# Attention scores as one fp32 product per head, and no splitting of q and k on GpSimd

## The reference

```python
def dilated_window_attention(q, k, v, window, dilation):   # q, k after rotary; 16 heads of 64
    r = window // (2 * dilation)                            # 64 for all three patterns
    # tokens are taken with a stride of `dilation`, each query sees keys at a distance <= 64 of them
    scores = jnp.einsum('nbqhd,nbkhd->nbhqk', qb, kw) * (HEAD_DIM ** -0.5)
    ...
    lse = jax.nn.logsumexp(scores, axis=-1)
    p = jnp.exp(scores - lse[..., None])
    o = jnp.einsum('nbhqk,nbkhd->nbqhd', p, vw)
    return o, lse

def dilated_mixture(q, k, v):
    # (window, dilation) = (128, 1), (512, 4), (2048, 16); merged with a softmax over the three lse
    ...
```

## Time and profile before

| What | us |
|---|---|
| median of three runs | 4509.62 |
| the profiled execution, its own time | 4508.95 |
| its span (first to last instruction) | 4507.3 |
| PE busy in the span | 4045.8 |
| POOL busy in the span | 1849.8 |
| attention, first to last score of TensorE | 2761.5 to 3883.2 |

### The profile page before, as it was taken

One profiled execution on the slowest core, in us unless ns is written; L12 is line 12 of the kernel. 1 busy time (PEld: TensorE's weight loads), 2 busy tenths in 40 slices (PEclk: granted clock), 3 DMA queues, 4 the chain that ended last, 5 costly groups with the idle time before them and its releaser, 6 DMA issues. The chain is left out here.

```text
span 4507.3 us, 61424 instructions
## 1 busy us (share of the span) xinstructions
PE 4045.8 (90%) x22213; PEld 3098.9 (69%) x22213; DVE 2337.4 (52%) x4451; ACT 1289.4 (29%) x3501; POOL 1849.8 (41%) x1135
## 2 busy tenths in 40 slices
PE   7999999999999999856777775999999999699999
PEld 5887778887788877623333334777777777588887
DVE  4402624205344026066888884666666666465654
ACT  1011220012120112101222223566566666422222
POOL 5453355443454533348999994111321121100000
PEclk9999999999999999978888887999999999899999
DMA  4232243231342322262222224334333343444442
GB/s 157 96 106 77 76 132 103 91 101 58 107 129 94 108 76 78 73 244 97 88 89 88 88 86 106 89 102 109 96 98 82 91 111 94 137 151 165 150 161 104
DMA packets 332021, 483.51 MB, mean 107 GB/s; under 512 B 27771, under 2 KB 228547, under 8 KB 329731
## 3 DMA queue, kind: packets, MB, share of 16 engines
q1 hardware_dynamic: 300867, 365.58, 25.5%
q0 software_dynamic: 26304, 94.78, 7.2%
q10 hardware_dynamic: 4608, 19.92, 1.3%
HBM read 315.04 MB, written 165.15 MB: 107 GB/s over the span
## 5 line engine op out<-in xcount | busy, mean ns | idle before, releaser
L253 POOL TENSOR_TENSOR front_w_hi<-front_w_raw,one 128x1024 fp32r<-128x1024 f32 (+1 forms) x168 | 302.6, 1801 | 932.9 <-PE front_out L475 920.4
L1487 ACT ACTIVATE attn_p_sb<-attn_p_sb,attn_o_sb 128x256 f32<-128x256 f32 (+1 forms) x1152 | 535.4, 467 | 388.1 <-DVE attn_o_sb L1520 388.1
L1520 DVE CUSTOM_DVE_ANT_0 attn_p_sb<-attn_s_ps,attn_mask 128x256 f32<-128x256 f32 (+1 forms) x1152 | 388.0, 374 | 91.1 <-PE attn_s_ps L1421 46.1
L256 POOL TENSOR_TENSOR front_w_lo<-front_w_raw,front_w_hi 128x1024 fp32r<-128x1024 f32 (+1 forms) x168 | 410.3, 2442 | 13.2
L406 DVE TENSOR_SCALAR front_acc<-front_chan,front_consts 128x1024 f32<-128x1024 f32 (+2 forms) x36 | 38.9, 1080 | 714.2 <-ACT front_chan L296 714.2
L475 PE MATMUL front_out<-front_h_hi,front_w_hi 128*128 128x512 f32 x1392 | 359.0, 401 | 8.9 <-DVE front_turned L386 3.6
L1421 PE MATMUL attn_s_ps<-attn_k_hi,attn_q_hi 64*128 64x256 f32 (+1 forms) x1152 | 283.6, 489 | 74.6 <-POOL attn_k_lo L1324 46.7
L475 PE MATMUL front_out<-front_h_hi,front_w_lo 128*128 128x512 f32 x1392 | 346.6, 391 | 0.0
L475 PE MATMUL front_out<-front_h_lo,front_w_hi 128*128 128x512 f32 x1392 | 344.2, 389 | 0.0
L1434 PE MATMUL attn_pt_ps<-ident,attn_p_sb 128*128 128x128 f32 x1920 | 339.9, 292 | 4.3 <-ACT attn_p_sb L1487 1.2
L960 PE MATMUL ssd_seg<-ssd_spread,masks 128*128 128x512 f32 x384 | 252.4, 800 | 95.5 <-POOL ssd_spread L899 95.4
(11 more groups left out here) (183 smaller groups left out, 7525.6 us busy)
## 6 DMA issues: line engine op xcount, KB each, us to landing
front_w_raw<-w_in POOLq DMA_DIRECT2D x156, 512.0 KB, 4.2
s_o<-attn_o_sb SPq DMA_DIRECT2D x288, 132.0 KB, 2.0
output_parts<-s_o SPq DMA_DIRECT2D x24, 1584.0 KB, 6.6
back_xb<-s_xb ACTq DMA_DIRECT2D x24, 640.0 KB, 6.3
ssd_xb<-s_xb SPq DMA_DIRECT2D x24, 640.0 KB, 3.9
s_q<-front_stage SPq DMA_DIRECT2D x48, 256.0 KB, 2.2
s_k<-front_stage SPq DMA_DIRECT2D x48, 256.0 KB, 2.3
s_zs<-front_stage SPq DMA_DIRECT2D x48, 256.0 KB, 3.5
```

The costliest lines, as they stand in the source:

```text
L253: nc.gpsimd.tensor_tensor(hi, raw, one.to_broadcast([P, 2, cols]), ALU.mult).then_inc(sem["w_hi_ready"], 1)
L256: nc.gpsimd.tensor_tensor(lo, raw, hi.bitcast(F32), ALU.subtract).then_inc(sem["w_split"], 1)
L1487: last = nc.scalar.activation(cut, cut, ACT.Exp, scale=-1.0, bias=o_sb[g // 2 % ring][:, g % 2, h, VW:OW], accum_out=o_sb[g // 2 % ring][: ...
L1520: last = nc.vector.tensor_tensor_reduce(out=p_sb[g % 3][:, h, 0:width], in0=s_ps[g % 2][h][:, 0:width], in1=mask[:, step.pattern.strip(ste ...
```

## The change

The score of a head becomes one fp32 product of q and k. The tiles `q_hi`, `q_lo`, `k_hi`, `k_lo` become `q` and `k`, the 192 split instructions on POOL and their two semaphores go, and TensorE waits, at the first step of a visit, for the 8 loads of q and k in place of the last split.

```diff
-        q_hi = [mem.sbuf(f"q_hi{u}", [P, longest], F32R) for u in range(2)]
-        q_lo = [mem.sbuf(f"q_lo{u}", [P, longest], F32R) for u in range(2)]
-        k_hi = [mem.sbuf(f"k_hi{u}", [P, longest + 2 * REACH], F32R) for u in range(2)]
-        k_lo = [mem.sbuf(f"k_lo{u}", [P, longest + 2 * REACH], F32R) for u in range(2)]
+        q = [mem.sbuf(f"q{u}", [P, longest]) for u in range(2)]
+        k = [mem.sbuf(f"k{u}", [P, longest + 2 * REACH]) for u in range(2)]
...
         def _(pool):
             for u in range(2):
-                for t in (k_hi[u], k_lo[u]):
-                    for at in (0, REACH + SEQS[1]):
-                        nc.gpsimd.memset(t[:, at:at + REACH].bitcast(F32), 0.0).then_inc(sem["a_pads_set"], 1)
+                for at in (0, REACH + SEQS[1]):
+                    nc.gpsimd.memset(k[u][:, at:at + REACH], 0.0).then_inc(sem["a_pads_set"], 1)
...
-            for part in range(len(split_parts(1))):
-                split(0, part)
             for step in steps:
-                following = step.visit + 1
-                if following < len(visits) and 0 <= step.at - 12 < len(split_parts(visits[following][0])):
-                    split(following, step.at - 12)
...
                 else:
-                    sp.wait_ge(sem["a_pads_set"], 8)
-                for name, tile, at in (("q", q_lo[u], 0), ("k", k_lo[u], REACH)):
+                    sp.wait_ge(sem["a_pads_set"], 4)
+                for name, tile, at in (("q", q[u], 0), ("k", k[u], REACH)):
...
                 if step.first_of_visit:
                     if step.visit == 0:
-                        pe.wait_ge(sem["a_pads_set"], 8)
-                    pe.wait_ge(sem["a_low"], splits_before(step.visit + 1))
+                        pe.wait_ge(sem["a_pads_set"], 4)
+                    pe.wait_ge(sem["a_qk_in"][u], 16 * 8 * (step.visit // 2 + 1))
...
-                for x, (qs, ks) in enumerate(((q_hi, k_hi), (q_hi, k_lo), (q_lo, k_hi))):
-                    for h in range(2):
-                        rows = slice(DH * h, DH * h + DH)
-                        last = nc.tensor.matmul(s_ps[g % 2][h][:, 0:width], pattern.columns(qs[u][rows, :], step.i),
-                                                pattern.columns(ks[u][rows, :], step.i, keys=True),
-                                                start=x == 0, stop=x == 2)
+                for h in range(2):
+                    rows = slice(DH * h, DH * h + DH)
+                    last = nc.tensor.matmul(s_ps[g % 2][h][:, 0:width], pattern.columns(q[u][rows, :], step.i),
+                                            pattern.columns(k[u][rows, :], step.i, keys=True),
+                                            start=True, stop=True)
                 last.then_inc(sem["a_scores"], 1)
```

More of the change, by code:

```diff
@@ L1266, in attention_phase @@
         block = stack.enter_context(nc.Block())
[L1267 to L1280, removed]
         def stored_upto(b, u):
@@ L1354, in load_qk @@
                             lane = DH * h + DH // 2 * a
-                            sp.dma_start(tile[lane:lane + DH // 2, at:at + SEQS[s]].bitcast(F32),
+                            sp.dma_start(tile[lane:lane + DH // 2, at:at + SEQS[s]],
                                          rows[pair // 2, 2 * (pair % 2) + h, a, :, first:first + SEQS[s]]
@@ L1880 @@
     "f_y_steps", "a_mask_steps", "a_odd_steps", "a_scores", "a_max", "a_exp", "a_p_turned", "a_outputs", "a_o_turned",
-    "a_ot_copied", "a_o_copied", "a_high", "a_low", "a_pads_set", "first_w_split",
+    "a_ot_copied", "a_o_copied", "a_pads_set", "first_w_split",
     "first_w_hi", "e_turned", "e_products", "e_w_hi", "e_w_split", "e_normed", "e_gain_in", "e_merged",
```

## The result

| What | before | after |
|---|---|---|
| median of 14 runs, us | 4510.64 | 4523.04 |
| profiled execution, its own time | 4508.95 | 4520.5 |
| its span | 4507.3 | 4518.9 |
| PE busy | 4045.8 | 4076.9 |
| POOL busy | 1849.8 | 1632.0 |

A forecast was written before the change was run, and what follows sets the result against it. TensorE was taken to bound attention (busy 99.6 of 100 us), except at the start and late stores. Terms 12 - 46 - 28 - 15 - 18 = -95 us took 4508.95 to 4414 us; range of 8 in 10: 4395 to 4530.

The forecast's parts named there:

- the first rival: Attention scores: a stride doubles the fp32 columns' cost, dilation 4 at 1.24 us a step; +3 us, 4512 us; chance 0.2.
- start: Start of attention: scores wait for loads alone, 19.9 us earlier, less 2 us waiting for a store; -18 us.
- dilation 1, the rest: Dilation-1 scores: 0.62 to 0.72 us a step, +18 over 192 steps, less 6 of hidden late stores; +12 us.
- dilation 4: Dilation-4 scores: 1.08 to 0.84 us a step if strided columns stay at two clocks; 192 steps, -46 us.
- dilation 16, long: Long sequence's dilation-16 scores: two weight loads in place of three, -0.22 us a step; 128 steps, -28 us.
- dilation 16, short: Short sequence's dilation-16 scores: the second pair goes, -0.24 us a step; 64 steps, -15 us.
- I take the lower one: Strided fp32 scores: of a lower and an upper cost bound, chose the lower, no extra stride cost over two clocks.
- The first score at 2742: Sign at the start of attention: first score about 2742 after the start, with no split on GpSimd.
- rival 2: Scores: two heads' fp32 products don't run side by side on halves of the rows; +141 us, 4650 us; chance 0.14.
- Dilation 1 at 0.72: Sign in a dilation-1 step: 0.72 us from its first score to the end of its last.
- the late store: Visit 0: the first store needed back is queued behind loads of v and next q and k; 2 us of waiting.
- Rival 3: VectorE and ScalarE hold shorter steps; half of dilation 16's gain lost gives 4435 us; no own chance, within forecast's range.

The follow-up runs named there:

- flat: Kernel after the change, but every step takes neighbouring columns of q and k (scores of other tokens, for timing only): 4403.76 us, ratio 0.9764.
- q_flat: Kernel after the change with neighbouring columns of q (the weights), the stride left in k: 4482.39 us, ratio 0.9937.
- k_flat: Kernel after the change with neighbouring columns of k (the moving operand), the stride left in q: 4430.87 us, ratio 0.9824.
- contig_ring: Kernel after the change, GpSimd copying strided q and k into side-by-side tiles, and ten output buffers for five: 4307.14 us, ratio 0.9552.
- b_flat: Kernel before the change (three fp32r products) with neighbouring columns of q and k in every step: 4413.2 us, ratio 0.9785.
- contig_spread: Kernel after the change, GpSimd copying strided q and k side by side, next visit's q and k loads issued one at a time: 4381.05 us, ratio 0.9705.
- contig_spread_ring: Kernel after the change with side-by-side copies on GpSimd, q and k loads issued one at a time, and ten output buffers: 4305.26 us, ratio 0.9549.

## Why the prediction was wrong, point by point

The measured time, 4523 us, lies inside the range of 8 in 10 (4395 to 4530), which had been drawn wide enough for the first rival; the forecast itself, 4414, had the wrong sign. The measured terms come from the distance between the first scores of neighbouring steps in the two traces, averaged over all steps of a pattern.

| Term | forecast, us | measured, us | from |
|---|---|---|---|
| start | -18 | -15 | first score 20.2 earlier; visit 0's dilation-1 steps 1.709 to 2.031, 16 steps, +5 |
| dilation 1, the rest | +12 | +8 | short 1.635 to 1.680, 64 steps, +3; long by +5 |
| dilation 4 | -46 | +39 | 2.213 to 2.417, 192 steps |
| dilation 16, long | -28 | -13 | 1.685 to 1.585, 128 steps |
| dilation 16, short | -15 | -8 | 1.842 to 1.718, 64 steps |
| sum | -95 | +11 | the span grew by 11.6 |

**The step that failed** is "I take the lower one, since the two clocks now may be the time of one access, which an fp32 matmul has anyway": a strided fp32 column was taken at the two clocks that a neighbouring one has. The runs show four: 0.45 us more for two passes of 256 keys (flat against q_flat). That is the term of dilation 4, -0.24 a step and -46 us, which measured +0.204 and +39: 85 us of the 106 between the two sums. The same price halves the dilation-16 terms, -21 us for -43: 0.69 us a step is what either stride alone gives, and the forecast had one of them only, the queries' weight loads. The first rival had it: 1.24, 0.80, and 4512 us, 11 under what came. Its sum of +3 against the +11 of the table is off by -4 at dilation 1, +8 at dilation 4, +1 at dilation 16 and +3 at the start. Its dilation 4 was 0.04 us short; the queries' stride costs 0.14 us a step in an fp32 product (k_flat against flat), and likely only a part of that was in the first pair that the forecast carried over, which no run separates.

The bound was at hand: every row of a strided operand of the kernel before, keys as well as queries, showed more time a column than its neighbouring kind. None showed a free stride. The nearest rows argued for the doubling, and an idea of why it might vanish was given more weight.

The Trainium skill (FP8 and Floating Point Precision, TensorE Precision Notes) gives true fp32 four passes through the array. Read with the stride paid in each pass, this case agrees: the product's four clocks a column become eight, and it pays 0.58 us a step for strides, where three fp32r products pay 0.46. The note on cachelines of another page of the Trainium skill (SBUF — State Buffer) asks for two hits on a 16-byte line; a stride of 4 fp32 elements gives one, and 1.28 against 0.70 us a step agrees.

**What was right.** The first score at 2742 (2741.3), with the loads as what ends the wait. The pairing of the two heads, so rival 2 (4650 us) falls: 0.70 us for four matmuls of 256 neighbouring columns is less than the 0.86 of four in a row at 0.215 each, half of what 512 columns take. Dilation 1 at 0.72 (0.70). The two weight loads a head. That all splits but the first visit's were covered: 218 us less on GpSimd, of which only the 19 at the start were seen.

**What was off in size.** At the start 2 us were set down for the late store; it and the lower clock took 5. Both were named, and the term of -15 lies inside its bounds, -20 and -13.

**Rival 3**, a chain through VectorE and ScalarE that holds the shorter steps, isn't there: contig_ring runs its long dilation-16 steps at 1.275 us with TensorE busy all the time, where the kernel after has 1.58.

**Where the sign came from**, then: per key column and head, the change trades three matmuls of one clock each for two of two clocks each, 3 clocks for 4, and wins back a weight load and the start. With strides it trades three of two clocks for two of four, 6 for 8, so the clocks lost are twice as many. The strides cost the kernel after 0.58 us a step of dilation 4 and the kernel before 0.46, 0.12 apart, and 192 steps of that are 23 us. From the pair without strides (-9.4) to the pair with them (+12.4) it is 21.8, but that the two numbers agree is in part luck. Dilation 16 goes the other way: in the short sequence, from step to step, strides cost the kernel before 0.42 us (1.842 against 1.426 in b_flat) and the kernel after 0.35 (1.718 against 1.366 in flat), and in the last long visit 0.35 and 0.28, which over all steps is 10 us or more. So by this estimate the strides explain about half of the 21.8, and the stalls and the clock of the pair without strides the rest. Held against the +9.5 us with no waits for stores in either kernel, it puts the change without strides at about even or a few us faster; the kernel before was never run with neither strides nor waits for stores.

## What to carry to other kernels

Price a matmul by its passes times the clocks a column of its *operand layout*, and take a known layout penalty as paid in every pass until a run shows that it isn't. When splits or other work on a side engine go away, use the room to lay both operands side by side: with that and a longer store ring the kernel is 4.5% faster than before (3.6% faster than the kernel before with the same ring), and 0.3% slower without. Count a short stall of a busy TensorE at more than its length, since the clock behind it may be halved. Here more buffers cured the stalls in every kernel they were tried on, and spreading the loads did so, nearly, in one of two.

## What the runs showed of the hardware

- A moving fp32 column at a stride of 4 elements cost about four clocks against two side by side (0.45 us more for 2 x 256, q_flat against flat), and strided fp32 weights 0.14 us a step of two products (k_flat against flat).
- Two heads' fp32 products on the two halves of the rows overlap although each head's product is issued whole: four matmuls of 256 columns in 0.70 us, where four in a row would need 0.86 (half of 0.43 each).
- A wait of TensorE of 1.9 us was followed by a granted clock of 0.50 for at least 12 us, with TensorE busy 6.00 of 6.00 us in each stretch (contig_spread); in another visit of the same run waits of 1.9 us in all were not. TensorE waits 19.4 us for VectorE in that run, yet contig_spread_ring, which differs by the ten buffers alone, is faster by 1.6% of the time before, some 70 us.
- GpSimd's strided copies, 11.2 us for four pieces each of q and k of dilation 4 (contig_ring), ran beside TensorE without slowing it: 0.49 us for the scores of a dilation-16 step, with the copies and without.
